# Last block of a decoder trunk: residual adds and norm steps moved from VectorE to GpSimd, one closing step moved back

## What is computed

```
h   = rms_norm(x, g_norm) * (1 + scale) + shift          # scale, shift, gate from a conditioning vector
p   = h @ w_in                                           # 3584 columns: h_A B_A C_A z_A u_B v_B z_B
y_A = B_A * dwconv3(C_A * h_A) * silu(z_A)               # 512 channels
y_B = u_B * (tril(W_s) layer_norm(v_B) + b_s) * silu(z_B)   # chunks of 128 positions, 512 channels
out = rms_norm(x + gate * ([y_A | y_B] @ w_out), g_final)
```

## Time and profile before

| | |
|---|---|
| median of 3 runs | 345.98 us (345.92 to 346.61) |
| profiled execution | 344.56 us |
| its span (first to last instruction, slowest core, core 1) | 342.7 us |
| PE busy | 292.4 us, 85% of the span |
| DVE busy | 187.3 us, 55% |
| ACT busy | 122.0 us, 36% |
| POOL busy | 110.5 us, 32% |
| last DVE instruction group (L781 x2) | starts 335.80 us, takes 1.41 us |

### The profile page before, as it was taken

The page is one execution under the profiler, slowest core; times in us unless marked ns, Lnnn a source line. Parts: engine busy times, 40 slices in busy tenths (PEclk is TensorE's granted clock), DMA queues, the critical chain, the costliest instruction groups (busy, mean ns, idle before and its releaser), DMA issues.

```text
span 342.7 us, 5627 instructions; the slowest of 8 cores (340.1 to 342.7 us)
## 1 busy us (share of the span) xinstructions
PE 292.4 (85%) x1792; PEld 152.2 (44%) x1792; DVE 187.3 (55%) x350; ACT 122.0 (36%) x215; POOL 110.5 (32%) x161
## 2 busy tenths in 40 slices
PE   0326549997899999999999999999999999999840
PEld 0213224443444445444455454446555557765410
DVE  0321016355553554737778836468853666667982
ACT  2611024118442234723445262443415244232320
POOL 7292244223323531412226342121432112222210
PEclk9999859999899999999999999999999999999995
DMA  5999999999999994193132816211180102527223
GB/s 163 211 149 178 159 160 163 166 192 261 211 197 168 148 155 106 32 249 122 62 82 103 182 66 148 61 63 62 63 221 25 33 0 105 142 69 196 89 111 122
DMA packets 14156, 44.50 MB, mean 130 GB/s; under 512 B 1968, under 2 KB 2352, under 8 KB 13104
## 3 DMA queue, kind: packets, MB, share of 16 engines
q0 software_dynamic: 6624, 21.24, 34.6%
q1 hardware_dynamic: 7504, 22.91, 24.2%
HBM read 51.02 MB, written 8.85 MB: 175 GB/s over the span
## 4 chain that ended last, share of the span: by engine, by line
PE 63%; DMA 23%; DVE 5%; issue 3%; POOL 2%; ACT 1%; DVEq 1%; POOLq 0%; ACTq 0%
PE pb L477 38%; PE pb L704 14%; DMA xa<-x_p 12%; DMA wada<-wada_l 11%; PE pb L592 7%; PE pb L403 1%; PE pb L656 1%; DVE ob L802 1%; PE pb L814 1%; POOL xa L314 1%; ACT junk L378 1%; DVE xn L389 1%; DVE ob L720 1%; DVE ob L721 1%; POOL wh L352 0%
## 5 line engine op out<-in xcount | busy, mean ns | idle before, releaser
L477 PE MATMUL pb<-hT,win_bf 128*128 128x512 bf16 (+3 forms) x680 | 127.4, 344 | 0.0
L477 PEld LDWEIGHTS pb<-hT,win_bf 128*128 128x128 bf16 x680 | 66.5, 98 | 56.1 <-issue 2.0
L704 PE MATMUL pb<-wout_bf,yT 128*128 128x512 bf16 (+1 forms) x256 | 58.1, 379 | 2.0 <-POOL yT L676 1.2
L477 PE MATMUL pb<-hT,wh 128*128 128x512 bf16 (+3 forms) x280 | 54.9, 357 | 2.8 <-DVE hT L423 2.8
L676 POOL TENSOR_TENSOR yT<-tmp,tmp 128x512 bf16<-128x512 f32 (+3 forms) x20 | 22.0, 1099 | 68.6 <-DVE tmp L666 39.2
L551 POOL TENSOR_TENSOR yT<-tmp,tmp 128x512 bf16<-128x512 f32 (+3 forms) x20 | 23.7, 1187 | 59.1 <-DVE tmp L546 41.0
L733 ACT ACTIVATE junk<-ob 128x1024 bf16<-128x1024 f32 (+1 forms) x16 | 16.9, 1057 | 72.3 <-DVE ob L723 59.9
L477 PEld LDWEIGHTS pb<-hT,wh 128*128 128x128 bf16 x280 | 27.9, 100 | 27.9 <-issue 8.1
L532 DVE SCALAR_TENSOR_TENSOR tmp<-spad,pv,tmp 128x512 f32<-128x512 f32 (+2 forms) x40 | 26.7, 667 | 20.4 <-ACT tmp L525 13.1
L704 PEld LDWEIGHTS pb<-wout_bf,yT 128*128 128x128 bf16 (+1 forms) x256 | 24.0, 99 | 29.6 <-issue 2.7
L592 PE MATMUL pb<-wv_bf,hT 128*128 128x512 bf16 (+1 forms) x136 | 30.3, 379 | 0.0
(11 more groups left out here) (88 smaller groups left out, 261.7 us busy)
## 6 DMA issues: line engine op xcount, KB each, us to landing
y_p<-ob SPq DMA_DIRECT2D x15, 512.0 KB, 2.7
xc<-x_p SPq DMA_DIRECT2D x14, 512.0 KB, 7.7
wada<-wada_l POOLq DMA_DIRECT2D x6, 1024.0 KB, 34.6
xa<-x_p POOLq DMA_DIRECT2D x10, 512.0 KB, 40.1
win_bf<-win_l POOLq DMA_DIRECT2D x17, 256.0 KB, 43.2
xa<-x_p SPq DMA_DIRECT2D x8, 512.0 KB, 6.8
wout_bf<-wout_l POOLq DMA_DIRECT2D x2, 1024.0 KB, 60.6
wh<-winh_l POOLq DMA_DIRECT2D x4, 256.0 KB, 26.7
```

The source lines that it names most:

```text
L477: ii = pe.matmul(bk.t[:, 0:B.N], lhsT=wsl(m, k), rhs=hT[B.h][:, k, 0:B.N], start=(k == 0), stop=(k == 7))
L704: ii = pe.matmul(bk.t[R, :], lhsT=yT[B.y][:, k, ti * 128:ti * 128 + P], rhs=wout_bf[:, n, k, :], start=(k == 0), stop=(k == 7))
```

## The change

`C_s1` gets a parameter for the engine of the residual add, `C_s2` one for the engine of its first small instruction. In the last block both go to POOL for the three old tiles and own tile 0. The closing step `C_s3` of old tile 2 moves from behind `GB(B, 3)` to behind the gate of own tile 0 (it is placed after `C_mm_half(B, 1, 0)`, which is PE work). `C_sq(B, 0)` keeps its place on ACT in front of the squares of own tile 1. Own tile 1 is unchanged.

```diff
-    def C_s1(B, i, sq=True):
+    def C_s1(B, i, sq=True, add="dve"):
...
-        op("dve", lambda e: e.tensor_tensor(out=o[R, :], in0=o[R, :], in1=xt[R, :], op=ALU.add),
+        op(add, lambda e: e.tensor_tensor(out=o[R, :], in0=o[R, :], in1=xt[R, :], op=ALU.add),
            r=[ores, xr], w=[ores])
...
-    def C_s2(B, i):
+    def C_s2(B, i, eng="dve"):
...
-        op("dve", lambda e: e.tensor_scalar(out=rs, in0=ss, scalar1=1.0 / D, scalar2=EPS, op0=ALU.mult, op1=ALU.add),
+        op(eng, lambda e: e.tensor_scalar(out=rs, in0=ss, scalar1=1.0 / D, scalar2=EPS, op0=ALU.mult, op1=ALU.add),
...
                 if j > 0:
-                    C_s2(PV, j - 1)
+                    C_s2(PV, j - 1, "pool")
                 if j < npv:
                     C_mm(PV, j, 0, 8)
-                    C_s1(PV, j, False)
+                    C_s1(PV, j, False, "pool")
...
-                elif j < 4:
+                elif j < 3:
                     C_s3(PV, j - 1)
...
-            C_s1(B, 0)
+            C_s1(B, 0, False, "pool")
             C_mm_half(B, 1, 0)
+            C_s3(PV, 2)
+            C_sq(B, 0)
             C_end1(B, 1, 0)
-            C_s2(B, 0)
+            C_s2(B, 0, "pool")
```

## The result

The changed kernel takes 348.32 us, median of 5 runs, against 345.92 us for the kernel before: ratio 1.0074, 95% interval 1.0058 to 1.0091, so 2.4 us slower by the medians and 2.6 by the ratio. The profiled execution took 347.88 us with a span of 346.3 us.

The account below looks back on a forecast made before the run. From 315.2 us on core 1 is bound by DVE's list; with POOL's adds and L802 excluding each other DVE ends 2.4 us later, so 344.56 becomes 347.0 profiled, plus 1.42 gives 348.4 us median; range 347.0 to 349.6, widened to 345.4 to 350.0.

Parts of the forecast that it names:

- The chain: Last block: POOL's adds hold L802, which delays the yT part and PE; DVE ends at 339.65 against 337.21, +2.4 us.
- The add's length on POOL: Moved 128x1024 add L723: 2.35 us on POOL, bounded by 2.2 and 2.5, against 1.23 on DVE.
- Exclusion: POOL's moved adds and DVE's L802 and L761 exclude each other; whoever comes second waits for nearly all of the first.
- The time hidden in a hold: DVE instruction held behind POOL hides 0.13 to 0.43 us of its own time; 0.35 taken for L802.
- Moved close: L802 of old tile 2 behind own tile 0's gate: gives back 0.9 us, then holds own tile 0's add to 333.14.
- The square: ACT's square with read-out, 1.2 us; own tile 0's counted with 0.33 us issue time, having started 0.43 after its input.
- rival 3: Forecast plus granted clock at half after PE idles before last yT part; some 2 us reach the end, 350.4 us; 5%.
- Rival 2: Adds are held or hold only in part; a third to two thirds of 3.6 us lost, 345.7 to 346.8 us; 7%.
- rival 1: No exclusion: POOL's add and L802 run side by side; DVE ends at 336.0, -1.2 us, 344.8 us; 12%.
- Rival 4: x for old tile 0 lands earlier: end at 338.9 instead of 339.65, at most 0.7 us; no chance of its own.

Follow-up runs that it names:

- the pair above: Changed kernel with 7 PSUM banks in turn, eighth filled with g_final: unread (control), ratio 1.0167; read by closing product L802, ratio 1.0040; both against kernel before.

## Why the prediction was right

I put the steps beside the trace, with 0.84 us taken off, by which the add of old tile 0 starts later in this execution (313.09 against 312.25).

| step | forecast | measured - 0.84 |
|---|---|---|
| add of old tile 1 starts | 316.92 | 316.86 |
| L802 of old tile 0 ends | 320.20 | 320.29 |
| yT part of step 2 ends | 321.83 | 321.89 |
| L802 of old tile 1 ends | 325.86 | 326.26 |
| yT part of step 3 ends | 327.49 | 327.85 |
| add of own tile 0 ends | 333.14 | 333.53 |
| L802 of own tile 0 starts | 336.01 | 336.39 |
| DVE ends | 339.65 | 339.96 |

- *The chain* is what the prediction said: POOL's add starts first, L802 behind it takes 3.23 us twice, the yT part and PE wait for that, and own tile 0's add is held in its turn.
- *The add's length on POOL*, 2.35 us from three shorter forms: 2.35 us. The Trainium skill's ratio of 1.96 ("GPSIMD Engine Reference", section 3.1) gives an estimate of 2.4 us for our 1.23; the measured ratio is 1.91.
- *Exclusion*: shown by the pair above. The Trainium skill's rule ("SBUF — State Buffer", "Who interferes with whom") is borne out here by both of its halves: with two SBUF inputs L802 takes 3.23 us under the add, with one 1.28.
- *The time hidden in a hold* was mis-sized: I took 0.35 us, it is 0.20 (321.13 against 320.05 + 1.28). Two holds in the chain make the 0.3 us by which the end came later than forecast. (The 0.43 that I read from L532 is 0.41 by its rows, 0.80 less 0.39.)
- *Moved close*: DVE's gate of own tile 0 follows PE as forecast (329.67 against PE's 329.43), and the add is held by the product in front of it, as forecast.
- *The square* of own tile 0 followed its add by 0.14 us, not 0.43; the 0.3 us saved went to L791, held by L761, which I had not counted.
- *The clock* (rival 3) did fall on core 1, and I had given it 5% and 2 us. In the windows of core 1 (columns as in the earlier trace rows) the granted clock is full while PE idles, then half:

```profile
326.30:328.80 2.50, 0.00 (x0) 0.00 (x0) 1.53 (x3) 1.02 (x2) 0.75 (x2) 1.00 0.32 128
328.80:330.00 1.20, 1.16 (x5) 0.52 (x6) 0.33 (x1) 0.00 (x0) 0.71 (x2) 0.91 0.47 184
330.00:332.00 2.00, 2.00 (x6) 0.76 (x5) 2.00 (x3) 0.00 (x0) 0.83 (x1) 0.50 0.00 0
```

The 16 matmuls of own tile 1 take 5.30 us on core 1. On core 0 they take 3.62 us, and yet both cores need the same 17.1 us from the start of old tile 2's add to the end of DVE (322.36 to 339.48, 323.67 to 340.80):

```profile
322.36 2.35 POOL L723 TENSOR_TENSOR ob<-ob,xc 128x1024 f32<-128x1024 f32 x1
...
327.53 0.59 PE L704 MATMUL pb<-wout_bf,yT 128*128 128x512 bf16 x2 [2.56 <-POOL yT L676]
327.96 3.62 PE L743 MATMUL pb<-wout_bf,yT 128*128 128x512 bf16 x16
...
338.07 1.41 DVE L781 SCALAR_TENSOR_TENSOR ob<-ob,stat,gf_bc 128x512 f32<-128x512 f32 x2 [0.80 <-POOL stat L776]
```

So on core 1 the drop was real and free: DVE waits for the first half only until 332.62, and its L761 would have been held by POOL's add anyway. It was not free everywhere. The same 16 matmuls take 5.2 to 5.3 us on cores 1, 2, 4, 5 and 6, 4.89 on core 3, and 3.62 on cores 0 and 7. On cores 3 and 5 the drop came early enough to slow the last two matmuls of own tile 0, which DVE's gate waits for:

```profile
328.27 1.01 PE L704 MATMUL pb<-wout_bf,yT 128*128 128x512 bf16 x2 [2.56 <-POOL yT L676]
329.07 4.89 PE L743 MATMUL pb<-wout_bf,yT 128*128 128x512 bf16 x16
```

That is core 3: 1.01 us instead of 0.59, and 17.54 us instead of 17.12 from old tile 2's add to the end (core 5: 0.74 and 17.27). Both have the longest span of this execution, 346.3 us, as core 1 has. So the rival's chance of 5% and its price of 2 us were both off: the drop came on six of eight cores and cost 0 to 0.4 us.

- *The prices of two rivals.* Rival 2 was added up wrongly: a third to two thirds of 3.6 us on top of rival 1's 344.8 give 346.0 to 347.2, not 345.7 to 346.8. Rival 4 said that late x moves the forecast by 0.7 us at most, but it followed the changed kernel alone: with early x in both, the ratios are 0.9953 and 1.0084, 4.5 us apart, since early x helps the kernel before and not the changed one.

The median moved by 2.4 us as forecast, though the chain's own growth on core 1 is 2.75 us by these steps (2.44 + 0.31) and the span's 3.6; the rest is ahead of the changed code, which is reached 0.7 us later in this execution (the gate L721 of old tile 0 starts at 310.32 instead of 309.63) and in which x comes 0.15 us later still. That the median hits 348.4 within 0.1 us is therefore in part luck: the profiled execution was forecast at 347.0 and took 347.88, and it lies 0.44 us under the median where the prediction carried over 1.42. What is not luck is the sign and the chain.

## What to carry to other kernels

Before moving an elementwise instruction from VectorE to GpSimd, list for both engines which instructions read two SBUF tensors: in these runs such pairs did not run side by side, whoever started first (3.23 us for L802 under the add, 3.20 for the add under L802), and the move then added GpSimd's longer duration to the chain instead of taking VectorE's off it. With one operand of the VectorE instruction in PSUM the pair ran freely here (1.28 and 2.36 us), but see what the bank costs: it ate the gain. And look first at an engine's wait for a DMA in front of its whole list: issuing the loads earlier gave the largest clear gain here.

## What was not expected of the hardware

- The granted TensorE clock went to half (the 1.2 GHz level, 0.50 in the windows) in the changed kernel on six cores after PE had idled 2.56 us between two groups of matmuls, and stayed at full (2.4 GHz) on cores 0 and 7 after an idle time of the same 2.56 us.
- Even POOL's 128x1 instructions are held: L791 took 0.54 us instead of 0.19 under DVE's L761, on all eight cores.
- A closing product of 128x1024 takes 1.28 us whether g_final comes from SBUF as float32 or from PSUM as bfloat16.
